# Both directions of a bidirectional gated recurrence in one tile per level, with one predicated copy per level, and the gate sigmoids issued inside the tail of attention

## What is computed

```
S_t = diag(f_t) S_(t-1) + k_t v_t^T        o_t = S_t^T q_t
f = lb + (1 - lb) * sigmoid(z)             k = (1 - lb) * sigmoid(-z)
```

## Time and profile before

| | us |
|---|---|
| median of 3 runs | 3350.36 (3344.38 to 3351.32) |
| profiled execution, its own time | 3349.04 |
| its span | 3347.3 |
| PE busy in the span | 3082.6 (92%) |
| DVE busy | 1785.2 (53%) |
| POOL busy | 1164.4 (35%) |
| ACT busy | 918.8 (27%) |

### The profile page before, as it was taken

One profiled execution on the slowest core, in us unless ns is written; L12 is line 12 of the kernel. 1 busy time (PEld: TensorE's weight loads), 2 busy tenths in 40 slices (PEclk: granted clock), 3 DMA queues, 4 the chain that ended last, 5 costly groups with the idle time before them and its releaser, 6 DMA issues. The chain is left out here.

```text
span 3347.3 us, 43291 instructions
## 1 busy us (share of the span) xinstructions
PE 3082.6 (92%) x16564; PEld 2336.7 (70%) x16564; DVE 1785.2 (53%) x2693; ACT 918.8 (27%) x1627; POOL 1164.4 (35%) x687
## 2 busy tenths in 40 slices
PE   7999999899999999999989999999957775998998
PEld 5888767677888788876757788877847755544444
DVE  6666735666666766673566666666257724011111
ACT  3222323442222322232244222233363321111110
POOL 3444344444444444434445444434334431000000
PEclk9999999999999999999889999999975786899999
DMA  5222220023222222222101322222200010699998
GB/s 190 95 94 94 76 104 29 1 76 112 96 94 94 80 105 98 94 75 95 39 1 57 113 95 94 94 92 95 76 38 1 1 57 38 280 424 425 426 426 340
DMA packets 40027, 411.30 MB, mean 123 GB/s; under 512 B 4432, under 2 KB 4688, under 8 KB 6992
## 3 DMA queue, kind: packets, MB, share of 16 engines
q1 hardware_dynamic: 39744, 408.02, 31.1%
q0 software_dynamic: 144, 1.38, 0.1%
HBM read 407.28 MB, written 2.10 MB: 122 GB/s over the span
## 5 line engine op out<-in xcount | busy, mean ns | idle before, releaser
L815 POOL TENSOR_TENSOR ffn_parts<-ring,ffn_parts 128x2048 fp32r<-128x2048 f32 x88 | 407.7, 4634 | 739.1 <-ACT ffn_parts L914 739.1
L2144 DVE SCALAR_TENSOR_TENSOR x<-banks,x 128x512 f32<-128x512 f32 x704 | 472.7, 690 | 301.5 <-PE banks L1676 301.2
L1856 PE MATMUL banks<-experts,tokens 128*64 128x256 f32 x2048 | 276.8, 386 | 47.8 <-DMA experts<-moe_w 45.4
L1856 PEld LDWEIGHTS banks<-experts,tokens 128*64 128x64 f32 x2048 | 151.5, 137 | 167.8 <-DMA experts<-moe_w 66.3
L1663 PE MATMUL banks<-x_parts_low,ffn_parts 128*128 128x512 f32 x672 | 264.3, 393 | 0.0
L1665 PE MATMUL banks<-x_parts_high,ffn_parts 128*128 128x512 f32 x672 | 264.3, 393 | 0.0
L1664 PE MATMUL banks<-x_parts_high,ffn_parts 128*128 128x512 f32 x672 | 264.1, 393 | 0.0
L1663 PE MATMUL banks<-h_lo,ffn_parts 128*128 128x512 f32 x672 | 262.3, 390 | 0.0
L1665 PE MATMUL banks<-h_hi,ffn_parts 128*128 128x512 f32 x672 | 261.4, 389 | 0.0
L1664 PE MATMUL banks<-h_hi,ffn_parts 128*128 128x512 f32 x672 | 261.4, 389 | 0.0
L914 ACT ACTIVATE ffn_parts<-ring 128x2048 fp32r<-128x2048 f32 x88 | 168.5, 1915 | 296.0 <-PE banks L1665 289.7
...
## 6 DMA issues: line engine op xcount, KB each, us to landing
experts<-moe_w SPq DMA_DIRECT2D x128, 1536.0 KB, 12.4
...
```

The costliest lines, as they stand in the source:

```text
L815: pool.tensor_tensor(s[:, 1], w, s[:, 0].bitcast(F32), ALU.subtract).then_inc(up_split, 1)
L1856: last = mm(o, xs[:, k, half], w[:, k], start=k == 0, stop=k == KC - 1, skip_group_check=True)
L2144: V.scalar_tensor_tensor(x[:, q], bank[4 + q % 4], scale, x[:, q], ALU.mult, ALU.add).then_inc(down_used, c.one(down_used))
```

## The change

The keys of both directions now lie in one tile and the queries in another: for level w the left halves hold the forward keys and the right halves the backward keys (`LEVEL_KEYS`), while `LEVEL_QUERIES` holds q times its factor for every token. One 128x128 by 128x128 matmul per block then gives both directions at once, together with pairs that belong to neither; one predicated copy of 128x512 per level, with one mask of 128x128 repeated over the four blocks, keeps the valid ones. ACT writes each half of the exponentials where the new layout wants it, in as many instructions as before. The levels use banks 2 and 3 alone. The diagonal copy is one instruction too. The two waits of the off-diagonal matmuls for earlier copies move: PE no longer waits for the last level's copy before them, nor for the copies L1322 and L1323 between levels, only before the head's product with the values.

The sigmoids move into attention's loop on ACT: `gates` is called in each step behind the last exponential, ahead of the step's PSUM copy. The barrier behind attention goes on all engines; DVE waits for attention's last matmul instead. `STAGES_BEFORE_ROUTER` falls from `LAYERS + 5` to `LAYERS + 4`, and the masks in `table` are 7 blocks of 128 columns in place of 14 of 64.

```diff
--- before.py
+++ after.py
@@ -120,12 +120,10 @@
         mult += (dist % dil == 0) & (dist <= window // 2)
     d[:, C2_DIST:C2_DIST + 896] = dist
     d[:, C2_MULT:C2_MULT + 896] = np.where(mult > 0, np.log(np.maximum(mult, 1)), NEG)
-    for back in range(2):
-        for n, m in enumerate(LEVELS):
-            blk = np.arange(64) // m
-            half = (p % (2 * m) >= m) if back else (p % (2 * m) < m)
-            at = C2_LVL + (back * len(LEVELS) + n) * 64
-            d[:, at:at + 64] = (p[:, None] // (2 * m) == blk[None]) & half[:, None]
+    t = np.arange(P)
+    for n, w in enumerate(LEVELS):
+        apart = (p[:, None] // w != t[None]// w) & (p[:, None] // (2 * w) == t[None] // (2 * w))
+        d[:, C2_LVL + n * P:C2_LVL + (n + 1) * P] = apart
     return c, d
 
 
@@ -330,7 +328,7 @@
     BC = [pair(prob.rearrange("p b n -> p (b n)")[:, 520 * d:520 * d + 516], NT) for d in range(2)]
     DD = [probT, pair(more[:, 0:1024], 2)]
     EE = [view(5120, 2 * T, a=2), pair(more[:, 1024:2048], 2)]
-    MM = [view(4096, 2 * T, a=2), pair(more[:, 2048:3072], 2)]
+    LEVEL_KEYS, LEVEL_QUERIES = view(4096, 2 * T, a=2), pair(more[:, 2048:3072], 2)
     QT = [view(16896, T, a=NT), pair(more[:, 3072:3584], NT)]
     KT = [view(17408, T, a=NT), pair(more[:, 3584:4096], NT)]
     QX = [pair(sq.rearrange("p b n -> p (b n)")[:, 384 * d:384 * d + 384], 3) for d in range(2)]
@@ -1069,7 +1066,7 @@
                 if n + 1 < FFN_ITEMS:
                     down_high(base, n + 1)
 
-        def attention(pairs, PT, highs=()):
+        def attention(pairs, PT, highs=(), behind=None):
             steps = NT * len(pairs)
             turns, sums = c.at.get(pT_ready.name, 0), c.at.get(pv_ready.name, 0)
             for a in range(steps + VALUES + 9):
@@ -1087,6 +1084,8 @@
                         src = PROBS[:, a % 4, e, 0:n] if u["bias"] is not None else SCORES[a % 2][:, e, 0:n]
                         act.activation(PROBS[:, a % 4, e, 0:n], src, ACT.Exp, bias=NM[:, 2 * (a % 2) + e:2 * (a % 2) + e + 1],
                                        accum_out=DEN[:, by:by + 1]).then_inc(probs_ready, 1)
+                if behind and a >= steps:
+                    behind(a - steps)
                 t = a - TURN
                 if 0 <= t < steps and pairs[t // NT]["bias"] is not None:
                     act.wait_ge(pT_ready, turns + 2 * t + 2)
@@ -1279,18 +1278,17 @@
             c.skip(down_used, (FFN_ITEMS - 1) * KC)
         second_inputs(base_second)
         meet(act, c, "act")
-        attention(dilated_pairs(), turned_keys(base_second + SECOND_ITEMS - 1))
-        meet(act, c, "act")
-
-
-        for m in range(H_HEADS + 1):
+        def gates(m):
+            if 0 < m <= H_HEADS:
+                act.wait_ge(step_act, c.made(step_act))
+                for d in range(2):
+                    act.activation(Z[d][:, m - 1], Z[d][:, m - 1], ACT.Sigmoid).then_inc(forget_ready, 1)
             if m < H_HEADS:
                 for d in range(2):
                     act.activation(K2[d][:, m], Z[d][:, m], ACT.Sigmoid, scale=-1.0).then_inc(step_act, c.one(step_act))
-            if m:
-                act.wait_ge(step_act, c.made(step_act, lag=2 if m < H_HEADS else 0))
-                for d in range(2):
-                    act.activation(Z[d][:, m - 1], Z[d][:, m - 1], ACT.Sigmoid).then_inc(forget_ready, 1)
+
+        attention(dilated_pairs(), turned_keys(base_second + SECOND_ITEMS - 1), behind=gates)
+
         for m in range(H_HEADS):
             for d in range(2):
                 act.wait_ge(forget_gated, c.next(forget_gated))
@@ -1312,10 +1310,11 @@
                     act.wait_ge(diff_ready, c.next(diff_ready))
                     if n == 0:
                         act.wait_ge(qk_ready, c.next(qk_ready))
-                    act.wait_ge(lvl_ready, c.next(lvl_ready, 1, lag=4))
-                    for src, dst, sign in zip(halves(DD[d][:, n % 2], w), halves(EE[d][:, n % 2], w), (-1.0, 1.0)):
-                        last = act.activation(dst, src, ACT.Exp, scale=sign)
-                    last.then_inc(decay_ready, 1)
+                    if d == 0:
+                        act.wait_ge(lvl_ready, c.next(lvl_ready, 1, lag=2))
+                    left, right = halves(DD[d][:, n % 2], w)
+                    act.activation(halves(EE[d][:, n % 2], w)[0], left, ACT.Exp, scale=-1.0)
+                    act.activation(halves(EE[1 - d][:, n % 2], w)[1], right, ACT.Exp).then_inc(decay_ready, 1)
                 if n == 0:
                     for d in range(2):
                         act.wait_ge(off_ready, c.next(off_ready))
@@ -1769,32 +1768,28 @@
         meet(pe, c, "pe")
         attention(dilated_pairs(), turned_keys(base_second + SECOND_ITEMS - 1))
         pe.drain().then_inc(attended, 1)
-        meet(pe, c, "pe")
 
         for m in range(H_HEADS):
             for d in range(2):
                 pe.wait_ge(qk_ready, c.next(qk_ready))
-                pe.wait_ge(off_copied, c.next(off_copied, 0))
-                pe.wait_ge(lvl_put, c.next(lvl_put, 0))
+                pe.wait_ge(off_copied, c.next(off_copied, 1, lag=1 + d))
                 for n, (I, J) in enumerate(PAIRS[d]):
                     q = QT[d][:, I] if n < 3 else QX[d][:, n - 3]
                     last = mm(bank[4 * d + n // 3][:, P * (n % 3):P * (n % 3) + P], KT[d][:, J], q, start=True, stop=True)
                 last.then_inc(off_ready, 1)
             for n, w in enumerate(LEVELS):
-                for d in range(2):
-                    pe.wait_ge(lvl_ready, c.next(lvl_ready))
-                    if n == 0 and d == 1:
-                        pe.wait_ge(off_copied, c.next(off_copied, 2))
-                    pe.wait_ge(lvl_put, c.next(lvl_put, 1, lag=4))
-                    for i in range(NT):
-                        blk = MM[d][:, n % 2, P * i:P * i + P]
-                        last = mm(bank[2 + 2 * d + n % 2][:, 64 * i:64 * i + 64], blk, halves(blk, w)[1 - d], start=True, stop=True)
-                    last.then_inc(lvl_mm, 1)
+                pe.wait_ge(lvl_ready, c.next(lvl_ready))
+                pe.wait_ge(lvl_put, c.next(lvl_put, 1, lag=2))
+                for i in range(NT):
+                    s = slice(P * i, P * i + P)
+                    last = mm(bank[2 + n % 2][:, s], LEVEL_KEYS[:, n % 2, s], LEVEL_QUERIES[:, n % 2, s], start=True, stop=True)
+                last.then_inc(lvl_mm, 1)
                 if n == 2:
                     pe.wait_ge(keys_ready, c.next(keys_ready, 2))
                     for i in range(NT):
                         last = mm(bank[6][:, P * i:P * i + P], KSUM[:, i], HQ[:, m, P * i:P * i + P], start=True, stop=True)
                     last.then_inc(diag_mm, 1)
+            pe.wait_ge(off_copied, c.next(off_copied, 0))
             pe.wait_ge(diag_put, c.next(diag_put))
             pe.wait_ge(head_out, c.next(head_out, 1, lag=1))
             for I in range(NT):
@@ -2286,9 +2281,9 @@
         second_inputs()
         meet(dve, c, "dve")
         attention(dilated_pairs(), turned_keys(base_second + SECOND_ITEMS - 1))
-        meet(dve, c, "dve")
-
-
+
+        dve.wait_ge(pT_ready, c.next(pT_ready, 0))
+        dve.wait_ge(pv_ready, c.next(pv_ready, 0))
         for d in range(2):
             V.memset(BC[d][:, :, 0:1], 0.0)
         for m in range(H_HEADS):
@@ -2322,42 +2317,32 @@
             for d in range(2):
                 V.tensor_scalar(QX[d][:, 2], QX[d][:, 1 - d], ET[d][:, 1 + d:2 + d], None, ALU.mult).then_inc(qk_ready, 1)
 
-            def product(n, d):
-                w = LEVELS[n]
-                dve.wait_ge(decay_ready, c.next(decay_ready))
-                e, o = halves(EE[d][:, n % 2], w), halves(MM[d][:, n % 2], w)
-                left, right = (q, k[d]) if d else (k[d], q)
-                V.tensor_tensor(o[0], halves(left, w)[0], e[0], ALU.mult)
-                V.tensor_tensor(o[1], halves(right, w)[1], e[1], ALU.mult).then_inc(lvl_ready, 1)
-
-            def put(n, d):
-                w = LEVELS[n]
+            def product(n):
+                w, at = LEVELS[n], n % 2
+                for d in range(2):
+                    dve.wait_ge(decay_ready, c.next(decay_ready))
+                    V.tensor_tensor(halves(LEVEL_KEYS[:, at], w)[d], halves(k[d], w)[d], halves(EE[0][:, at], w)[d], ALU.mult)
+                V.tensor_tensor(LEVEL_QUERIES[:, at], q, EE[1][:, at], ALU.mult).then_inc(lvl_ready, 1)
+
+            def put(n):
                 dve.wait_ge(lvl_mm, c.next(lvl_mm))
-                at = C2_LVL + (d * len(LEVELS) + n) * 64
-                mask = table[:, at:at + 64].bitcast(I32).rearrange("p (j w) -> p j w", w=w)
-                o = AT.rearrange("p i (j w) -> p i j w", w=2 * w)
-                o = o[:, :, :, 0:w] if d else o[:, :, :, w:2 * w]
+                at = C2_LVL + n * P
+                mask = table[:, at:at + P].bitcast(I32).unsqueeze(1).to_broadcast([P, NT, P])
                 dve.wait_ge(lvl_put, c.made(lvl_put))
```

(20 more changed lines are left out.)

5 lines of the change are left out of this document (2 added, 3 removed).

## The result

| | before | after |
|---|---|---|
| median of four runs, us | 3350.53 (3344.38 to 3351.32) | 3313.9 (3313.22 to 3315.23) |
| profiled execution, us (span) | 3349.04 (3347.3) | 3313.22 (3311.5) |
| the heads' levels, us | 131.05 | 103.77 |
| stretches between and behind heads, us | 35.35 | 32.45 |

The ratio of the runs is 0.989 (0.9878 to 0.9903): the change takes 36.6 us off, between medians, where 29 to 30 were forecast.

What follows compares the result with a forecast made beforehand. Bound: DVE's products alternating with POOL's subtractions in early levels, PE at 1.2 GHz in late ones. From 3349.04 us, levels -24.9, start -5.1 and gaps +1 gave 3320 us, range 3309 to 3332.

Steps and rivals of the forecast that it cites:

- Copy: DVE's eight masked copies per level become one of 128x512: 1.24 us becomes 0.62, bounds 0.54 and 0.89.
- Rival 4: The wide predicated copy on DVE is slower: break-even at 1.8 us a copy, 3365 us at 2.5; chance 0.03.
- Level matmuls: On PE, eight records of 128 moving columns replace 8 + 8: 1.71 to 1.82 us a level, half of 3.42.
- rival 3: Level matmuls on PE: 128 moving columns take twice what 64 take, so only DVE gains: 3347 us; chance 0.03.
- Early levels: While POOL makes its 14 subtractions, each DVE product waits out one: four levels of 3.85 us, 15.4 a head.
- Rival 5: Early levels: the 128x512 product stretches POOL's 14 turns over five levels, 1.8 us longer per head: 3327 us; chance 0.10.
- Late levels: With POOL done, three levels per head are bound by DVE: 2.05 us each, 6.2 together.
- Rival 1: PE's clock never rises in the recurrence: late levels 2.1 us each, gaps 4.4 longer: 3324 us; chance 0.17.
- Gaps: Stretches between and behind heads: 35.35 us stays if PE's clock rises as before, otherwise up to +4.4; taken as +1.
- Rival 2: PE's clock rises earlier and stays, shortening the stretches between heads: 3311 us; chance 0.12.
- The start: Ahead of the first head's level 0: attention ends 2.9 us later, scans start 2.6 earlier, level 0 5.1 earlier; bounds -2.6, -7.
- Behind the recurrence: The experts' stage begins earlier by what the recurrence saves and keeps its length, so each us saved counts at the end.

Runs made afterwards that it cites:

- e3: Changed kernel with the wide predicated copy written as four of 128x128 per level; median 3319.14 us, ratio 0.9907 to the kernel before.
- e5: Changed kernel with each level matmul of 128 moving columns split into two of 64; median 3339.68 us, ratio 0.9969 to the kernel before.
- e4: Changed kernel with the 512-wide query product split into two of 128x256; median 3325.96 us, ratio 0.9929 to the kernel before.
- e6: Changed kernel with four unread 512-column matmuls on PE before each head's wait for the diagonal copy; median 3310.89 us, ratio 0.9878 to the kernel before.
- e7: Changed kernel with POOL's second pair of first-head level subtractions waiting for DVE's scaled queries and keys; median 3315.65 us, ratio 0.9898 to the kernel before.
- e8: Changed kernel with DVE's gate scalings ahead of its wait for attention's last values; median 3315.3 us, ratio 0.9897 to the kernel before.

## Why the prediction was right, and where its terms were off

The time fell in the range, below the forecast by 6 us, and the case forecast (DVE the bound of late levels, POOL's alternation in early ones, a copy of 0.62) is the one that happened. That the number came so near owes something to luck: the clock's part and the start's were both off, in opposite directions.

**Copy: right.** 0.72 to 0.73 long and 0.62 to the next start, as taken. Rival 4, the dear copy, is false; e3 shows besides that a dearer one is paid in late levels only (0.17 more per copy gave 2.7 us over 28 copies, not 4.8).

**Level matmuls: right, and rival 3 false.** Eight records of 128 columns go by in about the time of eight of 64: e5's 64 records of 64 columns take 0.215 us each, and the change's PE time fell from 20.98 to 13.25 us in the third head, at PEclk 0.70 and 0.68 (in the second head, where it fell by half, the clock had risen as well). The Trainium skill's page "TensorE: Matmul & The Clock Gate", under "Back-to-back issue gap", has the gap of a lone matmul about double from 64 to 128 columns; for matmuls that each come with a weight load, as these do, it has no figure at 64, and from 0.215 to 0.23 us is all the growth that the traces show.

**Early levels: right.** Four of them, 15.2 us together for the 15.4 forecast, if not 3.85 each. Rival 5 is false: POOL's 14 turns fit as laid out. e4 shows where the rule behind it (each product waits out a turn) stops: at POOL's 14.

**Late levels: mis-sized.** The step "1.27 + 0.62 and some 0.15 of waiting for PE's 1.7 to 1.8, 2.05 each" measured 1.89. The 0.15 was a wait for PE at 1.2 GHz. It did not come up, since the clock rose in mid-head, behind the diagonal, in all four heads, and the records were done in 1.16 us; no run shows wide matmuls at 1.2 GHz beside copies of this speed through the late levels. Rival 1, the clock that never rises, is false. The third and fourth heads came out at 26.10 and 23.47 against 26.4 and 24.5, the first at 28.12 against 28.8.

**Gaps: wrong sign.** The step "I take +1, because full-width matmuls keep PE no busier per head and the clock may rise a little later" measured -2.9. The mean PEclk over the four heads' levels rose from 0.62 to 0.70, and in three of four gaps the same matmuls ran faster: 9.15, 9.20 and 3.84 against 10.24, 9.50 and 5.51. Rival 2 is true in part: the gaps went 2.9 us of the 9.2 that lie between 35.35 and e6's 26.1 with the clock up throughout. The term for a clock that never rises was a little small too: it takes 6.8 us for the last 32 records, by the price of 64 columns, where 1.82 for eight gives 7.3, and e3's took 6.61 at PEclk 0.56. Within the levels the clock rose at the same place in each head of the changed kernel and of e7 and e8, in the first group behind the diagonal. What decides where in a gap it rises stays open: e7 moved that by moving the start 1.5 us.

**The start: mis-sized.** The step "POOL then reaches the first head's subtractions while DVE is already at its factors' products, of which fewer wait the full 1.45" was wrong: more of them wait. Attention's end (+2.50), the scans (-3.06) and the first factor (E + 21.64 for E + 26.87, 5.2 earlier) came out near the forecast, but level 0 gained only 3.81 of 5.1. Before, the first of the four factor products ran free and of the scalings only the first was long:

```profile
2505.65 0.69 DVE L2314 TENSOR_TENSOR mix<-mix 128x512 f32<-128x512 f32 x1 [2.76 <-ACT mix L1306]
2511.61 0.27 DVE L2320 TENSOR_SCALAR sq<-mix,small 128x128 f32<-128x128 f32 x1
```

In the changed kernel POOL's key sum and subtractions come later against DVE's products. The first products take 1.07 and 1.76 us, and the second scaling 1.09: 7.59 us from the first product to the third scaling, where it was 6.16. Those 1.4 us are the missing amount, and e8, where the first product takes 0.69 and the second scaling 0.27 again, is back at 6.16. e7 gets its 1.5 us from the two scalings, of which the first had been long before the change too.

**Behind the recurrence: right.** The experts' stage is 462.0 long. The 2.1 us that the part behind is shorter are within what it varies by.

The stretch's -34.0 against the forecast's -29 is -2.4 from the levels, -3.9 from the gaps and +1.3 from the start: an error of the clock, in the main, partly cancelled by one of contention. For the gaps e6 shows that it is the clock; for the levels it is read from the trace alone.
